# One decoder step on one core: small copies of the short convolution on GpSimd, softmax scaling on ScalarE, sampled attention's first loads placed earlier

## The chip, the core and the metric

The kernel is one program for one core of one Trainium2 chip. Its time is the device time of one execution, in microseconds (us), and the measure is the median of several executions. The engines are TensorE (PE in the profile, its weight loads PEld), VectorE (DVE), ScalarE (ACT), GpSimd (POOL) and SyncE (SP, which here only issues DMAs). Each runs its own queue in order and waits for the others by semaphores. All data are float32.

## What is computed

One inference step of one layer, for a prompt of 512 tokens and for 8 sequences with 4 new tokens each (32 rows), so 544 columns in all. Cut to what matters here:

```python
h = rms_norm(x, norm1_w) * (1 + scale1) + shift1
(z, xbc, dt, q, k, v, qi, ki, wi, gb, gc, hv, gates) = split(h @ w_in)
y_a, conv_new, ssm_h = ssd_mixer(z, xbc, ...)           # depthwise conv of 4 taps on xbc, SiLU, scan
y_b = attend(q, k, v, qi, ki, wi)                       # index scores, top-k keys, softmax + relative bias
u, sc_new = causal_dwconv(gc * hv, sc_prev, sc_conv_w)  # short conv: 3 taps, two old rows in front
y_c = gb * u
merged = sum(sigmoid(gate) * (y @ w_out))
...                                                     # residual, second norm, 32 experts, final norm
```

For the prompt the keys are the 512 tokens. For the new tokens they are 1024 old ones, kept in pages of 128 rows that a page table names, and the new ones. `sc_new` is the last two rows of `gc * hv` of each sequence, an output; so is `conv_new`, the last three rows of `xbc`.

## The kernel before

Activations lie transposed: 128 channels on the partitions, 544 columns (NT) along the row, of which 512 are the prompt and 32 the new tokens. `hT` holds the normed input as 8 such blocks. A weight tile (128 x 1024) holds the weights of 128 output channels; tiles come from HBM into a ring, in order, by SP.

**The long stage** makes the tiles of the short convolution (24: three for each of its eight groups m), of `xbc` (16) and of `z` (8). The first 40 are taken two at a time, w = 0 to 19 (`two_main`): four quarters of two tiles are multiplied by seven half products instead of eight, from sums of weights that POOL makes ahead (`weight_sum`, L384, four instructions of 128 x 512 for each w) and from sums of activations. Each half product is eight matmul rows in the profile (L362). ACT copies the first and the fifth product out (`first_out` L1063, `block_out` L1074 or L1076); DVE adds the others (`read_two` L1286, `read_four` L1266, `read_six` L1294, `read_seven` L1280). The seventh product, the last of a w, waits for `read_four`, since it takes the bank of PSUM that `read_four` frees. The z tiles (u = 40 to 47, `project`, L350) come one at a time.

In between stand other jobs, placed by hand by the number u of the tile (u = 2w and 2w + 1):

- Prompt attention: 32 units (query block, head), one at each tile from u = 6 (A0). Unit k: PE `qk` (L912) at u = k + 6; DVE `attend` adds mask and bias and takes the maximum (L1158, L1162, L1163); ACT exponentiates with the row's sum (L1135); DVE `normalise` at the next tile inverts the sum (L1169) and scales the row (L1170); PE `turn` (L921) transposes it one tile later, before the products of that tile; ACT copies out (L1123), PE `pv` (L932) multiplies.
- Selection on DVE: rounds of a maximum of 8 and a replacement (L1177, L1180), for the prompt at w = 0 to 6 and for the new tokens (32 x 1056 scores) from w = 7, as many for each w as `NEW_ROUNDS` says.
- The short convolution on DVE (`short`, L1212 to L1229), one group m after `read_two` of w = 2, 3, 5, 6, 8, 9, 11 and 12. It multiplies c and h into the row `cg` (L1212, L1215), copies the sequences' two old values in front (L1213), copies the new state out (L1217, L1218), then convolves (L1222, L1224) and multiplies by b (L1226, L1227).
- The convolution of `xbc` on DVE (L1196, L1199), with its prefixes and state copied by POOL (`fill_rows` L867 and L868, `save_rows` L877 and L878) and SiLU on ACT (L1096).
- The adaLN modulation on PE (L335) every sixth tile.

**Sampled attention** follows (PE L1434 to L1495). Two halves a of four sequences; 16 page units u of eight pages, K then V, in two buffers. Buffer 0 is loaded by SP, buffer 1 by POOL (`pages_in`), and unit 0 by POOL too. A load waits for `s_kvused`, the count of units used, which PE raises by 2 at the very start of this stage (so that the first two may come) and then by 1 for each unit. The page buffers lie where the last weight sums were. Between the units PE makes the short convolution's output products (`short_half`, L1434); ACT takes the sigmoid of their gate (L1511) and DVE multiplies (L1559). DVE begins the stage with a wait for the biases `snear`, which SP loads from `rel_dram` by four DMAs (L1394), after the convolution state, which lies in the same place, has been written out by ACT (L1144) at the end of the long stage.

## Time and profile before

| | us |
|---|---|
| median of 3 runs | 1441.66 |
| lowest, highest | 1440.3, 1447.06 |
| the profiled execution, its own time | 1446.04 |
| its span in the trace | 1444.3 |

| engine | busy us | share of the span |
|---|---|---|
| PE | 1306.4 | 90% |
| DVE | 765.9 | 53% |
| ACT | 234.6 | 16% |
| POOL | 254.9 | 18% |

The profile is of one execution. The long stage runs from about 180 us to 585 us, its z tiles from 520 us; sampled attention from 585 us to 740 us. A row of the timeline is a group of equal instructions: start, length (from the first's start to the last's end), engine, line, operation, output and input, shape, number; in brackets how long the engine stood idle before it and what released it. Where several engines wait in turn, the one with no idle row for long sets the pace. Instructions of one engine overlap a little, so the time that one takes from its engine is read from its start to the next one's start. PEclk is the granted clock of PE as a share of its full 2.4 GHz.

### The profile page before, as it was taken

The numbers are of one execution on the slowest core, as the hardware profiler recorded it, in microseconds if no ns is written. First come the engines' busy times: TensorE is split into PE (matmuls) and PEld (weight loads), VectorE is DVE, ScalarE is ACT, GpSimd is POOL, SyncE is SP. The second block draws the span as 40 slices with busy tenths as digits, with TensorE's granted clock in tenths as the row PEclk, the third lists the DMA queues.
The fourth block names the chain that finished last, engine by engine and source line by source line (L and its number), as shares of the span: only waits on it lengthen the run. The fifth ranks groups of instructions, "written<-read, shape, count | busy, mean of one in ns | idle before, by whom it ended". The sixth has DMA issues, their size and how long they took to land. (4 is left out here: it accounts for less than half of the span.)

```text
span 1444.3 us, 19365 instructions
## 1 busy us (share of the span) xinstructions
PE 1306.4 (90%) x6937; PEld 933.5 (65%) x6937; DVE 765.9 (53%) x1475; ACT 234.6 (16%) x514; POOL 254.9 (18%) x359
## 2 busy tenths in 40 slices
PE   5999999989999999999989988999999799787774
PEld 2787667667778778676767766888878633222223
DVE  1534689999988867010115557685567622111115
ACT  2201111111122222010122222410001300000001
POOL 0214333322423300321210002000001211111001
PEclk7899999999999999999999997999999889999995
DMA  9452233313323333655561111421245599999945
GB/s 368 154 109 86 89 126 117 117 59 117 117 77 111 114 104 104 204 177 176 181 226 44 30 44 72 167 73 59 88 132 251 194 404 419 419 420 419 419 175 186
DMA packets 65281, 250.87 MB, mean 174 GB/s; under 512 B 9802, under 2 KB 19434, under 8 KB 51978
## 3 DMA queue, kind: packets, MB, share of 16 engines
q1 hardware_dynamic: 48706, 213.40, 39.3%
q0 software_dynamic: 10112, 20.47, 4.2%
q10 hardware_dynamic: 6376, 15.83, 3.8%
q8 instruction: 56, 0.92, 0.3%
q14 instruction: 31, 0.25, 0.1%
HBM read 234.47 MB, written 22.91 MB: 178 GB/s over the span
## 5 line engine op out<-in xcount | busy, mean ns | idle before, releaser
L362 PE MATMUL psum<-arena 128*128 128x272 f32 x2184 | 517.4, 394 | 16.0 <-DVE arena L1266 12.5
L362 PEld LDWEIGHTS psum<-arena 128*128 128x128 f32 x2184 | 409.6, 189 | 119.7 <-issue 32.5
L384 POOL TENSOR_TENSOR arena<-arena 128x512 f32<-128x512 f32 x80 | 106.6, 1333 | 225.9 <-DMA arena<-in_weights 164.3
L2766 PE MATMUL psum<-arena 128*64 128x512 f32 x512 | 117.8, 605 | 24.5 <-DMA arena<-in_w_gu 22.1
L1434 PE MATMUL psum<-arena 128*128 128x272 f32 x512 | 123.1, 398 | 2.0 <-DVE arena L1559 2.0
L350 PE MATMUL psum<-arena 128*128 128x272 f32 x512 | 121.1, 397 | 1.0 <-DVE arena L2082 1.0
L1434 PEld LDWEIGHTS psum<-arena 128*128 128x128 f32 x512 | 96.4, 191 | 28.0 <-DVE arena L1559 6.5
L350 PEld LDWEIGHTS psum<-arena 128*128 128x128 f32 x512 | 98.0, 192 | 23.7 <-DVE arena L2082 1.7
L2766 PEld LDWEIGHTS psum<-arena 128*64 128x64 f32 x512 | 35.6, 136 | 96.0 <-issue 70.7
L2788 PE MATMUL psum<-arena 128*64 128x512 f32 x256 | 63.5, 640 | 18.9 <-issue 16.2
L1559 DVE TENSOR_TENSOR arena<-arena,psum 128x272 f32<-128x272 f32 x16 | 7.0, 439 | 136.3 <-ACT arena L1511 123.2
L2840 DVE TENSOR_TENSOR arena<-arena,psum 128x256 f32<-128x256 f32 x16 | 6.8, 422 | 133.1 <-ACT arena L2831 133.1
L1753 PE MATMUL psum<-arena 128*128 128x272 f32 x256 | 64.5, 406 | 2.9 <-PEq L206 2.9
L1180 DVE MATCH_REPLACE8 arena<-arena 32x1056 f32<-32x1056 f32 (+3 forms) x80 | 64.9, 817 | 0.0
L1177 DVE MAX8 arena<-arena 32x8 f32<-32x1056 f32 (+3 forms) x80 | 63.5, 827 | 1.3 <-DVE arena L745 0.3
L1753 PEld LDWEIGHTS psum<-arena 128*128 128x128 f32 x256 | 49.7, 198 | 13.6 <-issue 3.1
L2848 DVE TENSOR_SCALAR arena<-psum,arena 128x1024 f32<-128x1024 f32 x16 | 20.5, 1284 | 63.8 <-PE psum L2788 63.8
L592 POOL DMA_DIRECT2D arena<-in_pages_i x64 | 33.3, 521 | 118.9 <-issue 112.6
L384 DVE TENSOR_TENSOR arena<-arena 128x512 f32<-128x512 f32 x76 | 52.7, 693 | 2.6
L2731 POOL DMA_INDIRECT y_rows<-arena x16 | 16.0, 998 | 214.9 <-DVE arena L2848 214.9
L2788 PEld LDWEIGHTS psum<-arena 128*64 128x64 f32 x256 | 20.0, 145 | 52.4 <-issue 49.2
L2635 POOL TENSOR_TENSOR arena<-arena 128x544 f32<-128x544 f32 x6 | 9.3, 1544 | 228.0 <-ACT arena L2458 228.0
(381 smaller groups left out, 1504.7 us busy)
## 6 DMA issues: line engine op xcount, KB each, us to landing
arena<-in_weights SPq DMA_DIRECT2D x153, 512.0 KB, 4.6
arena<-in_w_gu SPq DMA_DIRECT2D x32, 2048.0 KB, 34.6
arena<-in_w_down SPq DMA_DIRECT2D x16, 2048.0 KB, 35.5
arena<-in_weights ACTq DMA_DIRECT2D x16, 512.0 KB, 4.1
arena<-in_pages_k POOLq DMA_DIRECT2D x40, 128.0 KB, 3.8
arena<-in_x SPq DMA_DIRECT2D x2, 2176.0 KB, 13.6
arena<-in_pages_v SPq DMA_DIRECT2D x32, 128.0 KB, 3.1
arena<-in_pages_v POOLq DMA_DIRECT2D x32, 128.0 KB, 3.3
```

What stands on the lines that cost most here:

```text
L350: mm = pe.matmul(out[:, h, :], lhsT=w_of(n, c), rhs=act[:, c, h * HALF:(h + 1) * HALF], start=(c == 0), stop=(c == DC - 1))
L362: mm = pe.matmul(out, lhsT=w[:, c * P:c * P + P], rhs=x[:, c, :], start=(c == 0 and not added), stop=(c == 3), skip_group_check=added or more)
L384: link(dve.tensor_tensor(sums[:, k], a, b, op))
L592: pool.dma_start(kidx[64 * a:64 * a + 64, bass.ds(b, 1), j * PAGE:(j + 1) * PAGE].rearrange("p a n -> p (a n)"), ins["pages_i"][bass.ds(of ...
L1177: dve.max(best8[0:s.shape[0], i, :], s).then_inc(s_top, 1)
L1180: dve.match_replace(s, best8[0:s.shape[0], i, :], s, CHOSEN).then_inc(s_top, 1)
L1434: mm = pe.matmul(psum[:, bank, 0:HALF], lhsT=w_of(n, c), rhs=act_of[:, c, h * HALF:(h + 1) * HALF], start=(c == 0), stop=(c == DC - 1))
L1753: mm = pe.matmul(psum[:, (2, 7)[k % 2], 0:HALF], lhsT=w_of(n, c), rhs=act_of[:, c, (k % 2) * HALF:(k % 2 + 1) * HALF], start=(c == 0), sto ...
L2731: pool.indirect_dma_start(out=y_rows, out_offset=bass.IndirectOffsetOnAxis(tab_i[:, p - XG:p - XG + 1], 0), in_=yst[:, k, :], in_offset=No ...
L2766: mm = pe.matmul(psum[CAP * e:CAP * e + CAP, 2 + k, :].rearrange("p (o f) -> p o f", o=2), lhsT=xgT[:, k, lo:lo + CAP], rhs=wv[:, e, c4], ...
L2788: mm = pe.matmul(psum[CAP * e:CAP * e + CAP, 4 + h, :], lhsT=actT[:, k, at:at + CAP], rhs=w_dn[:, e, f * D + h * 512:f * D + h * 512 + 512 ...
L2848: dve.tensor_scalar(yst[:, k, :].rearrange("p (a n) -> p a n", n=512), psum[:, 4:6, :], wtab[:, p:p + 1], None, ALU.mult).then_inc(s_yo, 1)
```

## The change

Three edits, and what they need:

1. **Short convolution.** The three small copies of `short` go to POOL. `prefix(m)` copies the old values in front of the row; DVE's product into the row waits for it (`s_cgpre`). `save_short(m)` copies the state out, after DVE has raised `s_cgrow` for the row; then POOL waits for the end of this `short` (`s_scd`) and makes the prefix of m + 2, which uses the same row buffer. Both stand in POOL's queue behind the weight sums of the next w. `s_fill` counts one less; ACT waits for the last state copy before it uses the buffers' place at w = 14.
2. **Probabilities.** `normalise` becomes `invert`: DVE keeps the reciprocal, ACT scales the row (an ACT copy with a scale for each partition), just before its exponential of the next unit, and raises `s_prob`. In `NEW_ROUNDS` one round moves from w = 17 to w = 19.
3. **Sampled attention.** PE raises `s_kvused` before tile 40 instead of at the start of the stage. ACT writes the convolution state at u = 43 instead of at the end, and asks for the biases itself at u = 46; SP does so no more.

```diff
+                def prefix(m):
+                    pool.tensor_copy(seq_new(cg[:, m % 2, :], SSEG_P, SSEG_S, 0, 2),
+                                     param("sc_prev").rearrange("p (m b k) -> p m b k", b=NB, k=2)[:, m]
+                                     ).then_inc(s_cgpre, 1)
+
+                def save_short(m):
+                    row = cg[:, m % 2, :]
+                    pool.wait_ge(s_cgrow, m + 1)
+                    pool.tensor_copy(sc_state[:, m, 0:2], row[:, SEQ:SEQ + 2])
+                    pool.tensor_copy(sc_state[:, m, 2:18].rearrange("p (b k) -> p b k", k=2),
+                                     seq_new(row, SSEG_P, SSEG_S, 4, 6)).then_inc(s_cgst, 1)
+                    if m + 2 < 8:
+                        pool.wait_ge(s_scd, m + 1)
+                        prefix(m + 2)
...
                     for i in range(4):
                         weight_sum(pool, main_tile(2 * w), sums_of(w), i, sum_link)
+                    if 0 < w - 1 <= XB_FIRST and (w - 1) % 3 != 1:
+                        save_short(2 * ((w - 1) // 3) - (0 if (w - 1) % 3 == 2 else 1))
...
+                pe.wait_ge(s_took3, 5 * N_SEVEN - 2)
+                pe.sem_inc(s_kvused, 2)
                 for u in range(2 * N_SEVEN, N_MAIN):
...
                     if w == HOME2:
                         act.wait_ge(s_scd, 8)
+                        act.wait_ge(s_cgst, 8)
...
+                    if 1 <= k <= NU:
+                        w = (A_UNITS[k - 1][0] + 1) * P
+                        act.wait_ge(s_esum, k)
+                        act.activation(sp4[:, (k - 1) % 3, 0:w], sp4[:, (k - 1) % 3, 0:w], ACT.Copy,
+                                       scale=esum[:, k - 1:k]).then_inc(s_prob, 1)
...
                     if u == 43:
                         queries_spread()
-                act.wait_ge(s_state, XBC)
-                act.dma_start(outs["conv"], conv_state).then_inc(s_convout, 16)
+                        act.wait_ge(s_state, XBC)
+                        act.dma_start(outs["conv"], conv_state).then_inc(s_convout, 16)
+                    if u == 46:
+                        act.wait_ge(s_convout, 16)
+                        for g in range(4):
+                            act.dma_start(snear[32 * g:32 * g + 32, :], slid(0, NS, 0, P + NS)).then_inc(s_nearl, 16)
...
-                def normalise(k):
-                    w = (A_UNITS[k][0] + 1) * P
-                    s = sp4[:, k % 3, 0:w]
+                def invert(k):
                     dve.wait_ge(s_exp, k + 1)
-                    link(dve.reciprocal(esum[:, k:k + 1], esum[:, k:k + 1]))
-                    dve.tensor_scalar(s, s, esum[:, k:k + 1], None, ALU.mult).then_inc(s_prob, 1)
+                    dve.reciprocal(esum[:, k:k + 1], esum[:, k:k + 1]).then_inc(s_esum, 1)
...
                     dve.wait_ge(s_first3, 2 * ((3 * m + 2) // 2) + 2)
-                    if m == 0:
-                        dve.wait_ge(s_fill, 1)
+                    dve.wait_ge(s_cgpre, m + 1)
                     dve.tensor_tensor(row[:, 2:2 + SEQ], c_[:, 0:SEQ], h_[:, 0:SEQ], ALU.mult)
-                    dve.tensor_copy(seq_new(row, SSEG_P, SSEG_S, 0, 2),
-                                    param("sc_prev").rearrange("p (m b k) -> p m b k", b=NB, k=2)[:, m])
                     link(dve.tensor_tensor(seq_new(row, SSEG_P, SSEG_S, 2, 6), by_seq(c_), by_seq(h_),
                                            ALU.mult))
-                    dve.tensor_copy(sc_state[:, m, 0:2], row[:, SEQ:SEQ + 2])
-                    dve.tensor_copy(sc_state[:, m, 2:18].rearrange("p (b k) -> p b k", k=2),
-                                    seq_new(row, SSEG_P, SSEG_S, 4, 6)).then_inc(s_cgst, 1)
+                    dve.sem_inc(s_cgrow, 1)
...
-                NEW_ROUNDS = (3, 2, 2, 3, 2, 2, 3, 3, 3, 3, 3, 2, 1)
+                NEW_ROUNDS = (3, 2, 2, 3, 2, 2, 3, 3, 3, 3, 2, 2, 2)
...
-                sp.wait_ge(s_convout, 16)
-                for g in range(4):
-                    sp.dma_start(snear[32 * g:32 * g + 32, :], slid(0, NS, 0, P + NS)).then_inc(s_nearl, 16)
...
-                pe.sem_inc(s_kvused, 2)
```

Below, the instructions as they stand in the engines' queues. `arena` is the whole SBUF buffer, `psum` all of PSUM; names in brackets are the semaphores waited for, by the program's names.

DVE, from `short` of w = 8 to the attention unit after it, before:

```order
L1212 TENSOR_TENSOR arena<-arena 128x512 [waits first_products_read3,products_read3]
L1213 COPY arena<-arena 128x8x2
L1215 TENSOR_TENSOR arena<-arena 128x8x4
L1217 COPY arena<-arena 128x2 [waits dve_link3]
L1218 COPY arena<-arena 128x16
L1222 TENSOR_SCALAR arena<-arena 128x560
L1224 SCALAR_TENSOR_TENSOR arena<-arena 128x560 [waits dve_link3] x2
L1226 TENSOR_TENSOR arena<-arena 128x512 [waits dve_link3]
L1227 TENSOR_TENSOR arena<-arena 128x32
L1286 TENSOR_TENSOR arena<-arena,psum 128x272 [waits dve_link3,half_products3]
L1266 TENSOR_TENSOR arena<-arena,psum 128x272 [waits products_read3]
L1169 RECIPROCAL arena<-arena 128x1 [waits exp_ready,products_read3]
L1170 TENSOR_SCALAR arena<-arena 128x256 [waits dve_link3]
```

and of the change:

```order
L1242 TENSOR_TENSOR arena<-arena 128x512 [waits sc_prefix_ready,first_products_read3,products_read3]
L1243 TENSOR_TENSOR arena<-arena 128x8x4
L1248 TENSOR_SCALAR arena<-arena 128x560 [waits dve_link3]
L1250 SCALAR_TENSOR_TENSOR arena<-arena 128x560 [waits dve_link3] x2
L1252 TENSOR_TENSOR arena<-arena 128x512 [waits dve_link3]
L1253 TENSOR_TENSOR arena<-arena 128x32
L1312 TENSOR_TENSOR arena<-arena,psum 128x272 [waits dve_link3,half_products3]
L1292 TENSOR_TENSOR arena<-arena,psum 128x272 [waits products_read3]
L1201 RECIPROCAL arena<-arena 128x1 [waits exp_ready,products_read3]
L1192 SCALAR_TENSOR_TENSOR arena<-psum,arena 128x256 [waits probs_turned,qk_ready]
```

The three copies and the scaling are gone; the convolution's scaling (L1248, before L1222) follows the row at once.

ACT in the z tiles, from u = 43 on, of the change (before, the two DMAs' places held nothing, and the state's DMA stood behind the last row):

```order
L1112 ACTIVATE arena<-arena 128x16 x15
L1174 DMA out_conv<-arena 128x432 [waits conv_state_saved]
L1105 ACTIVATE arena<-psum 128x544 [waits w_used]
L1121 ACTIVATE arena<-arena 128x568 [waits conv_state_saved,conv_ready] x2
L1105 ACTIVATE arena<-psum 128x544 [waits w_used]
L1121 ACTIVATE arena<-arena 128x568 [waits conv_state_saved,conv_ready] x2
L1105 ACTIVATE arena<-psum 128x544 [waits w_used]
L1121 ACTIVATE arena<-arena 128x568 [waits conv_state_saved,conv_ready] x2
L1178 DMA arena<-rel_dram 32x1x132 [waits conv_state_written]
L1178 DMA arena<-rel_dram 32x1x132 x3
L1105 ACTIVATE arena<-psum 128x544 [waits w_used]
L1154 ACTIVATE arena<-psum 128x512 [waits modulation_turned,w_used]
```

The state leaves three tiles before the biases are asked for, and both stand ahead of the last two tiles' outputs.

## Rows read from the trace of the kernel before

**Rows 1.** Waits of PE from 190 us on, then PE's timeline in the long stage.

```profile
PE psum L362 <- DVE arena L1266: 11.9, 8, 3.0
...
239.33 2.07 PE L362 MATMUL psum<-arena 128*128 128x272 f32 x8 [1.43 <-DVE arena L1266]
...
271.00 2.87 PE L362 MATMUL psum<-arena 128*128 128x272 f32 x8 [2.82 <-DVE arena L1266]
...
297.97 4.29 PE L362 MATMUL psum<-arena 128*128 128x272 f32 x16 [0.93 <-DVE arena L1294]
...
324.94 2.07 PE L362 MATMUL psum<-arena 128*128 128x272 f32 x8 [3.02 <-DVE arena L1266]
...
376.63 2.07 PE L362 MATMUL psum<-arena 128*128 128x272 f32 x8 [1.58 <-DVE arena L1266]
```

**Rows 2.** Windows: stretch, length, busy of each engine (count), granted clock, DMA.

```profile
272.00:277.00 5.00, 5.00 (x25) 1.91 (x24) 4.08 (x13) 0.78 (x3) 0.00 (x0) 0.66 0.36 102
```

**Rows 3.** Timeline of DVE in block w = 8.

```profile
316.92 1.33 DVE L1212 TENSOR_TENSOR arena<-arena 128x512 f32<-128x512 f32 x1
318.17 1.24 DVE L1213 COPY arena<-arena 128x16 f32<-128x16 f32 x1
...
319.54 1.21 DVE L1217 COPY arena<-arena 128x2 f32<-128x2 f32 x1
...
320.74 0.50 DVE L1222 TENSOR_SCALAR arena<-arena 128x560 f32<-128x560 f32 x1
321.27 1.64 DVE L1224 SCALAR_TENSOR_TENSOR arena<-arena 128x560 f32<-128x560 f32 x2
...
324.83 0.16 DVE L1169 RECIPROCAL arena<-arena 128x1 f32<-128x1 f32 x1
325.03 0.35 DVE L1170 TENSOR_SCALAR arena<-arena 128x256 f32<-128x256 f32 x1
325.30 0.42 DVE L1158 SCALAR_TENSOR_TENSOR arena<-psum,arena 128x256 f32<-128x256 f32 x1
```

**Rows 4.** Timelines: POOL's sums in w = 8; two DVE instructions elsewhere, under POOL.

```profile
315.08 5.64 POOL L384 TENSOR_TENSOR arena<-arena 128x512 f32<-128x512 f32 x4 [17.92 <-DMA arena<-in_weights]
...
217.74 2.53 DVE L1224 SCALAR_TENSOR_TENSOR arena<-arena 128x560 f32<-128x560 f32 x2
...
348.27 1.44 DVE L1170 TENSOR_SCALAR arena<-arena 128x256 f32<-128x256 f32 x1
```

**Rows 5.** Timeline of DVE: its idle rows, and a selection of w = 19.

```profile
277.35 0.29 DVE L1158 SCALAR_TENSOR_TENSOR arena<-psum,arena 128x128 f32<-128x128 f32 x1 [1.17 <-PE psum L912]
...
415.40 0.56 DVE L1158 SCALAR_TENSOR_TENSOR arena<-psum,arena 128x384 f32<-128x384 f32 x1 [0.55 <-PE psum L912]
...
506.22 1.23 DVE L1180 MATCH_REPLACE8 arena<-arena 32x1056 f32<-32x1056 f32 x1
...
517.56 0.44 DVE L1294 TENSOR_TENSOR arena<-arena,psum 128x272 f32<-128x272 f32 x1 [3.80 <-PE psum L362]
```

**Rows 6.** Timelines of PE at the start of sampled attention, and of POOL there.

```profile
596.25 1.85 PE L1464 MATMUL psum<-arena 128*32 128x256 f32 x16 [0.41 <-DMA arena<-in_pages_k]
600.08 9.13 PE L1434 MATMUL psum<-arena 128*128 128x272 f32 x32 [1.99 <-DVE arena L1559]
609.15 1.07 PE L1464 MATMUL psum<-arena 128*32 128x256 f32 x16
610.18 7.60 PE L1434 MATMUL psum<-arena 128*128 128x272 f32 x32
...
585.60 9.63 POOL L1380 DMA_DIRECT2D arena<-in_pages_k  x16 [63.64 <-PEq L1414]
```

**Rows 7.** Timeline of DVE at the start of sampled attention.

```profile
599.59 0.44 DVE L1559 TENSOR_TENSOR arena<-arena,psum 128x272 f32<-128x272 f32 x1 [13.07 <-DMA arena<-rel_dram]
```

**Rows 8.** Timeline of POOL: a prefix copy of `fill_rows`.

```profile
500.83 0.21 POOL L868 COPY arena<-arena 128x24 f32<-128x24 f32 x1
```

**Rows 9.** Timeline of ACT in block w = 8.

```profile
317.85 0.39 ACT L1123 ACTIVATE arena<-psum 128x256 f32<-128x256 f32 x1
```

More of the change, by code:

```diff
@@ L818, in build @@
             s_qz, s_qz0 = sem("q_spread"), sem("q_zeroed")
+            s_kvused = sem("pages_used")
+            s_nearl = sem("snear_loaded")
+            s_cgrow, s_cgpre = sem("sc_rows_ready"), sem("sc_prefix_ready")
+            s_esum = sem("sums_inverted")
+            snear = A.at(a_tmp + 4096 + KEYS + 1152, P + NS)
             qz = A.at(a_sc, KV, NB, 32)
@@ L879, in save_rows @@
                                          seq_new(xb[:, m, :], SEG_P, SEG_S, 4, 7)).then_inc(s_state, 1)
+                def prefix(m):
[11 more added lines that the diff above has]
+                        prefix(m + 2)
                 for i in range(2):
-                    last = pool.memset(cg[:, i, 0:2], 0.0)
-                last.then_inc(s_fill, 1)
+                    pool.memset(cg[:, i, 0:2], 0.0)
+                    prefix(i)
                 for w in range(N_SEVEN):
@@ L1190, in conv @@
                     if j in (0, 4, 12):
-                        dve.wait_ge(s_fill, {0: 2, 4: 3, 12: 4}[j])
+                        dve.wait_ge(s_fill, {0: 1, 4: 2, 12: 3}[j])
                     if j >= 2:
@@ L1245, in at_tile @@
                     if 1 <= k <= NU:
-                        normalise(k - 1)
+                        invert(k - 1)
                     if k == 0:
@@ L1349, in _ @@
                 gain_of(dve, link, 1, "norm2")
-            s_kvused, s_sl5, s_smax, s_sexp, s_sprob, s_st, s_stout, s_so, s_nearl = (sem(n) for n in (
-                "pages_used", "slogits_read", "smax_ready", "sexp_ready", "sprobs_ready",
-                "sprobs_turned", "sturned_out", "satt_out", "snear_loaded"))
+            s_sl5, s_smax, s_sexp, s_sprob, s_st, s_stout, s_so = (sem(n) for n in (
+                "slogits_read", "smax_ready", "sexp_ready", "sprobs_ready",
+                "sprobs_turned", "sturned_out", "satt_out"))
             s_kv0 = sem("first_pages_loaded")
@@ L1361, in build @@
             ptn = A.at(a_tmp + 4096 + KEYS + 1024, P, parts=NEW)
-            snear = A.at(a_tmp + 4096 + KEYS + 1152, P + NS)
             st5 = A.at(a_tmp + 4096 + KEYS + 1152 + P + NS, 4)
```

## The prediction

> **What bounds the kernel now.** I read the page first: TensorE (PE) is busy 90% of the span, so only its pauses can be won back. Then the timeline of PE through the long stage. It pauses inside blocks of two tiles, all but once before the last eight matmuls of a block: 1.08, 1.43, 2.82, 0.73, 0.93, 3.02, 1.09 and 1.58 us. L1294 of VectorE (DVE) releases the 0.93, L1266 the others and one of 0.15, 11.9 us in eight; five of the nine stand in [rows 1] as the pattern, beside that sum. Seven of the eight lie in blocks w = 2, 3, 5, 6, 8, 9, 11, which are the ones in which DVE does a `short`; the one of 0.93 us (w = 7) follows w = 6. After the pause of 2.82 us eight matmuls take 2.87 us, where the same eight take 2.07 us elsewhere, and the granted clock of 272 to 277 us is 0.66 (of 2.4 GHz; 1.0 around it): 5 x 0.34 = 1.7 us, of which I count 1.6 [rows 1, 2].
>
> The timeline of DVE says why. From 278 us to 415 us it has no idle row at all [rows 5]: DVE paces this stretch and PE waits for it whenever it falls behind. In `short` of w = 8, L1212 starts at 316.92 and the row sum is done only at 324.8 [rows 3]. Two tiny copies stand out: L1213 (128x16) takes 1.24 us and L1217 (128x2) 1.21 us, as long as one POOL sum of the weights, of which four run from 315.08 to 320.72 [rows 3, 4]. So the copies do not cost work, they wait for POOL's running instruction. POOL slows others too: L1224 twice takes 2.53 us under it and 1.64 us without, and the probabilities' scaling L1170 takes 1.44 us under it and 0.35 us without [rows 3, 4].
>
> The third view is PE at the start of sampled attention: it waits 0.41 us for pages and 1.99 us for DVE's L1559, which itself waited 13.07 us for the biases from `rel_dram`; around these pauses the clock is low (16 page matmuls 1.85 us instead of 1.07, 32 others 9.13 us instead of 7.60) [rows 6, 7].
>
> **The copies of `short` (eight times).** Off DVE go L1213, L1217 and L1218. From the start of L1213 to that of L1222 (318.17 to 320.74) [rows 3] are 2.57 us, of which L1215 keeps some 0.2, so 2.4 us at most. But the next instruction on DVE is now L1222, a scaling of SBUF data as L1170 is, and L1170 under POOL took 1.1 us more [rows 4]. I replay w = 8, in us from POOL's start, with its four sums ending at 1.3, 2.7, 4.0 and 5.3 or so. L1212 ends at 3.1 as now; L1222 waits until the third sum is done (4.0), runs to 4.5; the first L1224 shares its time with the fourth sum (+0.9, as in [rows 4]) and ends at 6.15, the second at 6.95. Now it ends at 321.27 + 1.64 - 315.08 = 7.8. The saving is 0.9 us, not 2.4. POOL's starts lie 0.8 to 3.4 us before L1212 in the other blocks, and the replay gives 0.8 to 1.0 for each. I take 0.9, with 0 (everything is passed on) and 2.4 as bounds.
>
> Here a rule of the Trainium skill bears on it, in SBUF — State Buffer, "Who interferes with whom": DVE and GpSimd share one pair of ports, a lock held for a whole instruction by whoever comes first, and copies, tensor_scalar and tensor_tensor with both inputs in SBUF all want it. The rows above agree (a 128x2 copy of 1.21 us). By that rule the edit only takes away customers of the lock, not the lock; a reader who prices the copies at their busy time would write 2.4 us per `short`.
>
> The copies on POOL cost it 0.21 us each by their nearest likes (L868, same shape but for the width) [rows 8]: 0.6 us for three, in a queue that stands idle 17.92 us before its next sums [rows 4]. Queued behind POOL's new waits (for the row, for the end of `short`) are the next weight sums; they start only when their tiles have landed and PE has finished two blocks back, after `short` is over. DVE's new wait, for the prefix, is met one `short` earlier. Zero on the path.
>
> **Scaling moved to ACT (32 times).** Off DVE goes the step L1169 to L1158: 324.83 to 325.30, 0.47 us, of which the reciprocal's own slot of 0.11 stays: 0.36 us [rows 3]. Narrow units give less (0.3), wide ones more. Two of them ran under POOL (the 1.44 of [rows 4] and one like it at the start of w = 4): 1.1 us more each. On ACT the scaling costs about what L1123 costs at the same width, 0.39 us [rows 9], and ACT is busy 16% of the span by the page. The path that could suffer is PE's transpose, which now waits for ACT: L1169 ends at 324.99, ACT +0.4, handing over +0.14, so 325.6; PE, released at 324.94 with 2.07 us of matmuls before the transpose [rows 1, 3], comes at 327.0. 1.4 us of slack, zero cost.
>
> **The sum in the long stage.** While DVE never idles, PE gains what DVE has saved since its last idle, but no more than the pauses so far.
> - w = 2: min(1.08, 0.9) = 0.9.
> - w = 3 and 5: DVE saves 0.9 + 0.9 + four scalings 1.4 + 1.1 contended = 4.3; PE can gain 0.9 at w = 3 and then 2.82: 3.7. The clock's dip goes with the long pause: 1.6.
> - w = 6 to 11, from DVE's idle at 277.35 [rows 5]: by w = 8 saved 2 x 0.9 + 4 x 0.36 = 3.2 (pauses so far 4.7); by w = 9 another 0.9 + 0.7 = 4.9; by w = 11 DVE has 8.3, PE gains 4.9 + 1.58 = 6.4.
> Together 12.6 us. With 2.4 per `short` all pauses go: 12.7 + 1.6 = 14.3. With 0 per `short`: 2.5 + 1.6 for w = 5 and 2.2 + 1.6 = 3.8 for the rest, 7.8 in all.
>
> The one selection round that moves from w = 17 to w = 19 costs nothing: it is a maximum and a replacement over 1056 scores, 1.23 us each or a little more [rows 5], 2.6 us in front of a DVE idle of 3.80 us [rows 5]; from w = 12 on PE has no pauses.
>
> **Pages and biases.** `s_kvused` is raised before tile 40, so POOL's sixteen page loads (9.63 us of issue [rows 6]) no longer wait 63.64 us for PE but start near 522 us, behind POOL's last copies; sixty microseconds cover them, and the buffers are free by the waits that stand before them. POOL's issues now run beside DVE's convolutions and may slow those; their results are due a tile later, and TensorE's eight tiles there have no pause for them. The convolution state is written at u = 43 and the biases asked for at u = 46, both on ACT's queue: four issues between one tile's output and the next, with a whole tile of PE to spare before anyone waits for ACT. SP loses four issues and a wait and comes to its pages earlier. PE's 0.41 + 1.99 go, and with them the clock's loss, 0.78 + 1.53 [rows 6]: 4.7 us. What comes late next is the second page unit's load by SP, released when unit 0 is done; before PE needs it come unit 1 and two halves of the short product, 7.6 us each [rows 6].
>
> **Sum.** 12.6 + 4.7 = 17.3 us. Of the profiled execution's own 1446.04 us 1428.7 are left. That execution lies 4.4 us over the median of the runs shown (1441.66); on the median's scale it is 1424.4 us.
>
> **Rivals.**
> - *Everything goes*: the copies' full 2.4 us are won since L1222 finds POOL no hindrance (for it: L1222 took 0.50 us each time so far [rows 3]; against it: L1170's 1.44). 14.3 + 4.7 = 19.0, 1422.7 us.
> - *The wait is passed on*: L1222 and both L1224 take over what the copies waited. For it speaks that POOL's four sums are as long as before and DVE's queue is full of instructions that they slow. 7.8 + 4.7 = 12.5, 1429.2 us. By the rule of SBUF — State Buffer in the Trainium skill, taken to its end, this is the case.
> - *Another wait at the start of sampled attention*: PE's pauses there stay, because ACT's queue or POOL's descriptors deliver late. 12.6 only, 1429.1 us.
> - *Slower*: PE's transposes wait for ACT. Each of 32 now has the chain reciprocal, ACT's scaling, PE, and ACT works in order, behind its own waits for PE's products. It decides once the chain passes 2.0 us where it is now some 0.6; at 1.2 us over, 32 x 1.2 = 38 us less the 17.3 gained give 1463 us. Against it: ACT is mostly idle in this stretch (L1123 of w = 8 is its last work for 8 us), and what stands ahead of the scaling on it has been released earlier.
> - *It does not do what it says* for the pages: POOL stays behind another wait. The order of its queue shows only the counters named, so this goes with the third.
>
> **How the numbers follow.** Forecast (1424.4) 0.57; everything goes 0.13; passed on 0.15; attention's pauses stay 0.08; slower 0.04, and no change to speak of, several of these at once, 0.03. The range holds the first four: from 1422.7 less 2 us, since the runs shown spread from 1440.3 to 1447.06, to 1429.2 and 2 us: 1420.5 to 1431.5. A measurement of this kernel can tell about 0.5% (7 us) from no change. Faster 0.92, same 0.04, slower 0.04.
>
> **What would show it.** Right: L1222's successor taking 1 to 1.5 us in several `short`s; PE pauses in the long stage of 1 to 3 us in all, none over 2; no low clock near 270 and 600 us; page loads from 522 us; DVE's wait for `rel_dram` gone; ACT's new scalings 0.3 to 0.6 us. Wrong: PE waiting for ACT's scaling before transposes; L1222 always at 0.50; pauses at new places, at w = 4 or 10; or a PE wait for pages of unit 0 or 2.

## The result and the profile after

The changed kernel takes 1438.07 us (median of 10 runs, 1431.3 to 1444.16) beside 1447.09 us for the kernel before in the same comparison (10 runs, 1440.3 to 1450.49): a ratio of 0.9943, interval 0.992 to 0.9966, so some 8 us (5 to 12) instead of the 17.3 forecast, and a time outside the range of 1420.5 to 1431.5 us. The profiled execution took 1438.11 us, its span is 1436.5 us; of before they were 1446.04 and 1444.3.

Where the 7.8 us between the two spans lie, by the first instruction of each stretch on PE:

| stretch | before | after | forecast | measured |
|---|---|---|---|---|
| start to the last product of w = 0 | 189.18 | 188.15 | 0 | -1.03 |
| from there to the first z matmul (long stage) | 330.90 | 327.72 | -12.6 | -3.18 |
| z tiles and sampled attention | 222.48 | 219.01 | -4.7 | -3.47 |
| the rest | 701.74 | 701.62 | 0 | -0.12 |

These are single profiled executions. A second one of the changed kernel (e8 below) has 326.61 us in the long stage, 217.56 in the third row and 706.99 in the rest, so the two gains measured lie between 3.2 and 4.3 us and between 3.5 and 4.9.

**PE's timeline in the long stage**, its rows that begin with idle time (start, length, instructions, in brackets the idle time and what ended it):

```profile
221.10 2.07 PE L362 MATMUL psum<-arena 128*128 128x272 f32 x8 [0.93 <-DVE arena L1292]
237.90 2.07 PE L362 MATMUL psum<-arena 128*128 128x272 f32 x8 [1.19 <-DVE arena L1292]
269.07 2.07 PE L362 MATMUL psum<-arena 128*128 128x272 f32 x8 [2.31 <-DVE arena L1292]
286.83 2.07 PE L362 MATMUL psum<-arena 128*128 128x272 f32 x8 [1.49 <-DVE arena L1292]
295.11 3.98 PE L362 MATMUL psum<-arena 128*128 128x272 f32 x16 [0.87 <-DVE arena L1320]
...
321.06 2.81 PE L362 MATMUL psum<-arena 128*128 128x272 f32 x8 [2.31 <-DVE arena L1292]
...
372.31 2.07 PE L362 MATMUL psum<-arena 128*128 128x272 f32 x8 [0.84 <-DVE arena L1292]
```

Nearly the pattern of [rows 1] is left, eight pauses of nine, 10.10 us in all where 12.83 were. Block by block: w = 2 gained 0.15, w = 3 0.24, w = 5 0.51, w = 7 0.05, w = 8 0.71, w = 9 all its 1.09, w = 11 0.74; w = 6 lost 0.76. Block by block this is not the edits' doing alone. The kernel e1 below has the instructions of before throughout this stage, and its profile shows 1.98 us of pause at w = 6 where before shows 0.73, and none at w = 7 and w = 9 (PE's timeline of e1, its rows from 285 to 345 us that begin with idle time):

```profile
288.36 3.58 PE L362 MATMUL psum<-arena 128*128 128x272 f32 x8 [1.98 <-DVE arena L1277]
...
324.11 2.07 PE L362 MATMUL psum<-arena 128*128 128x272 f32 x8 [3.08 <-DVE arena L1277]
```

**DVE's and POOL's timelines in block w = 8**, which answer to [rows 3, 4]:

```profile
313.00 0.69 DVE L1242 TENSOR_TENSOR arena<-arena 128x512 f32<-128x512 f32 x1
313.60 1.26 DVE L1243 TENSOR_TENSOR arena<-arena 128x32 f32<-128x32 f32 x1
315.01 1.45 DVE L1248 TENSOR_SCALAR arena<-arena 128x560 f32<-128x560 f32 x1
316.50 2.53 DVE L1250 SCALAR_TENSOR_TENSOR arena<-arena 128x560 f32<-128x560 f32 x2
319.07 0.69 DVE L1252 TENSOR_TENSOR arena<-arena 128x512 f32<-128x512 f32 x1
...
311.66 5.93 POOL L384 TENSOR_TENSOR arena<-arena 128x512 f32<-128x512 f32 x4 [17.37 <-DMA arena<-in_weights]
```

The waiting copies are gone, and two other instructions wait in their stead: the 128x32 product L1243 (L1215 before) takes 1.26 us instead of 0.18, the scaling L1248 (L1222 before) 1.45 us instead of 0.50. By shape, over all eight `short`s (DVE's groups of 205 to 400 us: busy us, mean ns of one, idle):

```profile
L1250 DVE SCALAR_TENSOR_TENSOR arena<-arena 128x560 f32<-128x560 f32 x16 | 16.4, 1025 | 0.6
L1248 DVE TENSOR_SCALAR arena<-arena 128x560 f32<-128x560 f32 x8 | 10.7, 1342 | 1.2 <-DVE arena L1243 0.2
L1243 DVE TENSOR_TENSOR arena<-arena 128x32 f32<-128x32 f32 x8 | 10.1, 1258 | 0.0
```

Best measured is the stretch from the start of the row's product (L1212, now L1242) to the start of the multiplication by b (L1226, now L1252), read from the timeline in each of the eight blocks w = 2, 3, 5, 6, 8, 9, 11, 12:

| kernel | us in each block | sum |
|---|---|---|
| before | 6.27, 5.65, 6.63, 5.41, 6.02, 6.36, 5.48, 4.79 | 46.6 |
| after | 6.11, 5.43, 6.98, 6.16, 6.07, 4.50, 6.07, 5.34 | 46.7 |

Three copies less, and the eight blocks are no shorter. The sums repeat within about 1 us: e1, with the copies, has 46.6 us again, e8, without them, 47.7. A single block varies more, with the moment at which DVE meets POOL's sums. w = 9 is 1.9 us shorter than before, and its pause is gone, but e1 has 5.42 us there and no pause either. w = 6 is 0.75 us longer, and its pause grew by 0.76, but e1 has 6.28 us there: in before this row's product starts 2.5 us behind POOL's first sum, in e1 1.3 us and in the changed kernel 1.5 us. There three instructions in a row wait (DVE's timeline, then POOL's):

```profile
278.67 1.66 DVE L1242 TENSOR_TENSOR arena<-arena 128x512 f32<-128x512 f32 x1
280.26 1.25 DVE L1243 TENSOR_TENSOR arena<-arena 128x32 f32<-128x32 f32 x1
281.66 1.46 DVE L1248 TENSOR_SCALAR arena<-arena 128x560 f32<-128x560 f32 x1
...
277.16 5.65 POOL L384 TENSOR_TENSOR arena<-arena 128x512 f32<-128x512 f32 x4 [8.98 <-DMA arena<-in_weights]
```

**Start of sampled attention**, timelines of PE, POOL and DVE:

```profile
591.55 1.66 PE L1483 MATMUL psum<-arena 128*32 128x256 f32 x16
593.14 8.66 PE L1453 MATMUL psum<-arena 128*128 128x272 f32 x32
...
525.51 9.68 POOL L1405 DMA_DIRECT2D arena<-in_pages_k  x16 [7.77 <-issue]
...
589.54 0.44 DVE L1578 TENSOR_TENSOR arena<-arena,psum 128x272 f32<-128x272 f32 x1 [7.24 <-ACT arena L1530]
```

And windows of the changed kernel (length; busy of PE, PEld, DVE, ACT, POOL with counts; granted clock; DMA share, GB/s):

```profile
267.00:272.00 5.00, 2.93 (x20) 1.76 (x24) 4.68 (x16) 1.18 (x4) 0.42 (x3) 1.00 0.00 0
321.00:327.00 6.00, 5.94 (x28) 2.76 (x29) 4.38 (x9) 1.39 (x4) 0.00 (x0) 0.72 0.33 85
592.00:605.00 13.00, 13.00 (x70) 9.24 (x63) 0.44 (x1) 0.40 (x1) 1.36 (x3) 0.87 0.42 126
```

Both pauses of [rows 6] are gone, the loads start 60 us earlier, and DVE waits no longer for `rel_dram` [rows 7]. But PE's first matmuls are slow still (1.66 for 1.07 us, 8.66 for 7.60): the clock was low here without any pause right before them (the last idle row of PE is 0.72 us at 580.51, and e1 and e8 have it too). In the long stage the low clock moved from w = 5 [rows 2] to w = 8; in e1 it comes behind the 1.98 us at w = 6 and not behind the 3.08 at w = 8, and in e8 not at all (1.00), with a pause of 2.49 us at w = 8.

### The profile page after: what moved, and what is told of

Read it like the earlier page. It is cut to its first block and busy times, and to the rows that moved or that the text cites. A ratio compares the mean times of both kernels' runs of the same rounds, so it can differ in the third digit from the quotient of the medians.

```text
span 1436.5 us, 19374 instructions
## 1 busy us (share of the span) xinstructions
PE 1303.0 (91%) x6937; PEld 929.0 (65%) x6937; DVE 749.8 (52%) x1419; ACT 250.2 (17%) x546; POOL 261.2 (18%) x383
## 5 line engine op out<-in xcount | busy, mean ns | idle before, releaser
L1772 PEld LDWEIGHTS psum<-arena 128*128 128x128 f32 x256 | 49.9, 199 | 13.7 <-issue 3.2
```

What stands on the lines that cost most here:

```text
L1772: mm = pe.matmul(psum[:, (2, 7)[k % 2], 0:HALF], lhsT=w_of(n, c), rhs=act_of[:, c, (k % 2) * HALF:(k % 2 + 1) * HALF], start=(c == 0), sto ...
```

## The experiments

Times are medians; ratios are to the kernel before, run beside each. L is the long stage, P the sum of PE's pauses in it from w = 2 on, S the z tiles and sampled attention, as in the table above. These three come from one profiled execution each. The kernel before was run anew with each set of experiments (medians 1447.55, 1445.89 and 1448.10), so the ratios and not the times are to be compared.

| kernel | us | ratio (95%) | L | P | S |
|---|---|---|---|---|---|
| before | 1447.09 | | 330.90 | 12.83 | 222.48 |
| after | 1438.07 | 0.9943 (0.992 to 0.9966) | 327.72 | 10.10 | 219.01 |
| e1_pages | 1443.35 | 0.9967 (0.995 to 0.9985) | 330.03 | 12.13 | 217.50 |
| e2_short | 1445.85 | 0.9987 (0.9964 to 1.001) | 330.05 | 12.21 | 224.64 |
| e3_scale | 1444.69 | 0.9982 (0.9964 to 1.0) | 328.93 | 11.42 | 221.70 |
| e4_late_sums | 1423.86 | 0.9845 (0.9801 to 0.9888) | 313.91 | 0.00 | 219.71 |
| e5_late_sums_old | 1434.54 | 0.9921 (0.9891 to 0.9951) | 317.57 | 2.54 | 223.95 |
| e6_late_pages | 1430.25 | 0.9881 (0.9849 to 0.9913) | 317.55 | 2.53 | 220.95 |
| e7_late_again | 1428.02 | 0.9872 (0.9847 to 0.9897) | 313.92 | 0.00 | 220.79 |
| e8_after_again | 1441.34 | 0.9957 (0.9937 to 0.9977) | 326.61 | 10.37 | 217.56 |
| e11_late_short | 1430.48 | 0.9872 (0.9849 to 0.9894) | 317.10 | 2.19 | 224.00 |
| e12_late_scale | 1431.21 | 0.9859 (0.982 to 0.9899) | 313.99 | 0.00 | 223.36 |

### Each edit alone

**e1_pages**: the third edit alone (the biases' part not shown).

```diff
+                pe.wait_ge(s_took3, 5 * N_SEVEN - 2)
+                pe.sem_inc(s_kvused, 2)
                 for u in range(2 * N_SEVEN, N_MAIN):
...
-                pe.sem_inc(s_kvused, 2)
```

> Only the third edit (pages and biases early), the rest as before. Measures in this and the other runs: L, the long stage, from the end of the pause of w = 0 to the first z matmul (before 330.9 us, after 327.7), the sum P of PE's pauses in it from w = 2 on (before 12.8, after 10.1), and S, from the first z matmul to the first matmul behind sampled attention (before 222.5, after 219.0). Theory (the three edits act in places of their own): L 330.9 and P 12.8 stay, S falls to 219.0. Rival (the loads in the z tiles disturb or help the long stage's end, or S needs the other edits): L moves by over 1 us or S stays above 221.

S falls by 5.0 us, both pauses are gone, and here the clock stays full (the same window as above, of e1):

```profile
592.00:605.00 13.00, 13.00 (x80) 9.20 (x79) 0.88 (x2) 0.40 (x1) 0.55 (x2) 1.00 0.36 102
```

Priced at 4.7, worth 5.0 where the clock stays up, and 1.5 us better than the 219.0 expected, which was the changed kernel's. L is 0.87 us and P 0.7 us less than in before, though no instruction of the long stage differs: so much two executions can differ there, and smaller differences in L or P prove nothing as long as POOL's sums run beside the `short`s. In the changed kernel the same stretch shows 3.5, and the difference is (1.66 - 1.07) + (8.66 - 7.60) = 1.65 us of slower matmuls. The same kernel run again (e8) has the clock at 1.00 there and S lower by 4.9.

**e2_short**: the first edit alone.

```diff
-                dve.tensor_copy(sc_state[:, m, 0:2], row[:, SEQ:SEQ + 2])
-                dve.tensor_copy(sc_state[:, m, 2:18].rearrange("p (b k) -> p b k", k=2),
-                                seq_new(row, SSEG_P, SSEG_S, 4, 6)).then_inc(s_cgst, 1)
+                dve.sem_inc(s_cgrow, 1)
...
+                    if 0 < w - 1 <= XB_FIRST and (w - 1) % 3 != 1:
+                        save_short(2 * ((w - 1) // 3) - (0 if (w - 1) % 3 == 2 else 1))
```

> Only the first edit (small copies of the short convolution on POOL). Theory (the wait for POOL's running sum is passed on): the 128x32 product takes 1.26 us instead of 0.18 and the scaling behind it 1.46 instead of 0.50, each short is at most 0.5 us shorter, P falls from 12.8 to 11 to 12.5. Rival (the copies gave most of the gain of the long stage, the scaling nothing): P 10 to 10.5, L 328.

P falls by 0.6 and L by 0.85 us where the forecast had 0.9 for each of eight. That is no more than e1 shows with nothing changed there. The eight stretches take 45.4 us instead of 46.6: 0.15 us each; the whole 1.2 us is hardly more than the 1 us by which such sums repeat. The wait came as expected: in all eight blocks the 128x32 product takes 1.25 to 1.26 us. The kernel's time can't be told from that of before.

**e3_scale**: the second edit alone.

```diff
-                    dve.tensor_scalar(s, s, esum[:, k:k + 1], None, ALU.mult).then_inc(s_prob, 1)
+                    dve.reciprocal(esum[:, k:k + 1], esum[:, k:k + 1]).then_inc(s_esum, 1)
```

> Only the second edit (probabilities scaled by ACT, one selection round moved). Theory (only what is saved inside a block with a short counts, some 0.4 us for each of six such blocks; what is saved in others becomes DVE idle before the next unit's logits): P falls from 12.8 by 2 to 3, to 10 to 11, and DVE shows new idle rows for PE's qk of 1 to 2.5 us in blocks without short. Rival (DVE paces the whole stretch, savings add up, as predicted): P falls by 5 to 8. Second rival (scaling on ACT gives nothing): P stays at 12.5 to 12.8.

L falls by 1.97 us, P by 1.41, so P misses the 2 to 3 expected, and of L 0.87 may be chance (e1). The interval of the time reaches 1. ACT does the work at 399 to 716 ns by width, and PE never waits for it before a transpose. But 32 scalings of 0.36 us would be 11.5 us of DVE. That they are not had is seen in DVE's idle rows. The kernel before has no idle row of DVE between 238.27 and 277.35 us, where [rows 5] begin. e3 has three there, 1.50, 0.84 and 0.17 us, and the changed kernel nearly the same; these are its rows:

```profile
248.66 0.44 DVE L1312 TENSOR_TENSOR arena<-arena,psum 128x272 f32<-128x272 f32 x1 [1.50 <-PE psum L362]
255.21 0.29 DVE L1192 SCALAR_TENSOR_TENSOR arena<-psum,arena 128x128 f32<-128x128 f32 x1 [0.85 <-PE psum L934]
273.79 0.29 DVE L1192 SCALAR_TENSOR_TENSOR arena<-psum,arena 128x128 f32<-128x128 f32 x1 [0.17 <-PE psum L934]
```

What DVE saves in w = 3 and 4 it now spends waiting for PE, ahead of the `short` of w = 5, whose length then sets the pause as before. Further on it is the same: before has no idle row from 277.35 to 415.40 us, the changed kernel has three there (and e3 2.41, 2.05 and 0.83 us):

```profile
327.95 0.43 DVE L1192 SCALAR_TENSOR_TENSOR arena<-psum,arena 128x256 f32<-128x256 f32 x1 [2.40 <-PE psum L934]
359.17 0.56 DVE L1192 SCALAR_TENSOR_TENSOR arena<-psum,arena 128x384 f32<-128x384 f32 x1 [2.10 <-PE psum L934]
377.90 0.56 DVE L1192 SCALAR_TENSOR_TENSOR arena<-psum,arena 128x384 f32<-128x384 f32 x1 [0.83 <-PE psum L934]
```

In e8, where the clock stays full at w = 8, the first of them is 0.77 us: part of the 2.40 is DVE waiting for a PE that is slow. In e3 the eight stretches are even a little longer, 47.6 us.

### GpSimd's sums kept out of the way

**e4_late_sums**: the changed kernel, but POOL makes the next weight sums only when the `short` beside which they ran is over. No DVE or ACT work is touched.

```diff
+                    if 0 < w - 1 <= XB_FIRST and (w - 1) % 3 != 1:
+                        m = 2 * ((w - 1) // 3) - (0 if (w - 1) % 3 == 2 else 1)
+                        save_short(m)
+                        pool.wait_ge(s_scd, m + 1)
                     for i in range(4):
                         weight_sum(pool, main_tile(2 * w), sums_of(w), i, sum_link)
-                    if 0 < w - 1 <= XB_FIRST and (w - 1) % 3 != 1:
-                        save_short(2 * ((w - 1) // 3) - (0 if (w - 1) % 3 == 2 else 1))
```

> The changed kernel with POOL's weight sums held back in the eight blocks with a short until that short is over (POOL saves the state rows first, then waits for the end of short, then sums). Theory (a lock between the two engines costs the time): in short the product 0.18, the scaling 0.50, the two convolution steps 1.64 and the row product 0.69 in all eight, a short some 3 us shorter than after (4.3 instead of 7 us), P falls from 10.1 to under 4, with at most 1 us of new pauses where PE waits for POOL's sums; L 320 to 323. Rival (DVE's own work bounds the blocks, not the contention): P 8 to 10, L 327. Second rival (held-back sums come late): new pauses before the second or fourth product of the next block of over 1 us each, P above 10.

Timelines of DVE and POOL in w = 8:

```profile
321.40 0.69 DVE L1244 TENSOR_TENSOR arena<-arena 128x512 f32<-128x512 f32 x1
322.01 0.18 DVE L1245 TENSOR_TENSOR arena<-arena 128x32 f32<-128x32 f32 x1
322.34 0.51 DVE L1250 TENSOR_SCALAR arena<-arena 128x560 f32<-128x560 f32 x1
322.89 1.64 DVE L1252 SCALAR_TENSOR_TENSOR arena<-arena 128x560 f32<-128x560 f32 x2
324.56 0.69 DVE L1254 TENSOR_TENSOR arena<-arena 128x512 f32<-128x512 f32 x1
...
325.63 5.39 POOL L384 TENSOR_TENSOR arena<-arena 128x512 f32<-128x512 f32 x4
```

DVE's groups by shape, as above:

```profile
L1245 DVE TENSOR_TENSOR arena<-arena 128x32 f32<-128x32 f32 x8 | 1.5, 184 | 0.0
L1250 DVE TENSOR_SCALAR arena<-arena 128x560 f32<-128x560 f32 x8 | 4.1, 515 | 1.2 <-DVE arena L1245 0.2
```

And PE's only wait from 189 to 503 us (total, times, longest), which is that of w = 0:

```profile
PE psum L362 <- DVE arena L1294: 0.6, 1, 0.6
```

Each stretch takes 3.16 to 3.18 us, 25.3 us for the eight instead of 46.7. PE has no pause left and L falls by 13.8 us, much more than the expectation had (320 to 323 for the 313.91 measured): the 10.10 of pauses, 1.6 us of low clock at w = 8 (eight products 2.81 instead of 2.07, the modulation after them 2.81 instead of 1.93), and some 2 us that show as the same matmuls being busy less long. Nobody waits for the later sums. This kernel is faster than both others; run again beside the changed one (e7 and e8) the intervals stay apart, 0.9847 to 0.9897 against 0.9937 to 0.9977.

> The changed kernel with held-back sums once more, timed in five rounds. Both theories of the mechanism expect its ratio to the kernel before at 0.980 to 0.987; if the first measurement of 0.9845 owed much to chance, 0.988 to 0.994.

> The changed kernel itself, unaltered, timed on the same chip as the others, for its clock and its pauses in a second profiled execution. Theory (the low clock at the start of sampled attention comes in some executions and not in others, whether or not PE pauses there): P 9.5 to 10.7 again, L 326 to 328.5, but S anywhere from 217 to 220. Rival (the low clock belongs to this kernel's order of work): S 219 again, with 8.6 us for the second run of 32 products instead of 7.6.

e7 comes out between its two expectations, e8 as its theory had it: pauses and L again (10.37 and 326.61 us), and S 217.56 us with a full clock.

**e5_late_sums_old**: the kernel before, with that wait alone. **e6_late_pages**: e5 and the third edit.

```diff
+                    if 0 < w - 1 <= XB_FIRST and (w - 1) % 3 != 1:
+                        m = 2 * ((w - 1) // 3) - (0 if (w - 1) % 3 == 2 else 1)
+                        pool.wait_ge(s_scd, m + 1)
                     for i in range(4):
                         weight_sum(pool, main_tile(2 * w), sums_of(w), i, sum_link)
```

> The kernel before with one edit alone: POOL's weight sums in the eight short blocks wait for the end of short. The small copies and the scaling stay on DVE, pages and biases stay late. Theory (it is the meeting of the two engines that costs, not who does the copies): each copy takes 0.17 us (some 1.2 before), L1224 0.80 each, a short is under 5 us, P falls from 12.8 to under 2, L from 330.9 to 313 to 316. Rival (the edits of the change are needed too, the gain of the held-back sums rests on the copies being off DVE): the two copies keep 1.2 us each, P 5 to 8, L 320 or more.

> The kernel before with the held-back sums and the third edit (pages and biases early), the copies and the scaling still on DVE. Theory: within 1 us of the changed kernel with held-back sums in L (313 to 315) and S (217 to 220): the first two edits then bring nothing. Rival: they still bring 2 us or more, L 316 or more.

The one wait takes 13.3 us from L, three to four times what the three edits of the change together took (3.2 and 4.3 us in its two profiles). e5's pauses (2.54 us for under 2) and its L (317.57 for 313 to 316) come out a little over what was expected. e6 misses its expectation that the first two edits bring nothing once the sums are held back: its L is 317.55 us and that of e4 313.91, as its rival had it. The copies with which the prediction began cost this (e5, groups by shape):

```profile
L1220 DVE COPY arena<-arena 128x2 f32<-128x2 f32 x8 | 1.4, 170 | 0.3
L1216 DVE COPY arena<-arena 128x16 f32<-128x16 f32 x8 | 1.4, 170 | 0.0
```

The eight stretches take 26.2 us. So 46.6 - 26.2 = 20.4 us in before, 2.55 us each, were waits for POOL. They show in the length of the copies, of the row's product and of the convolution, but go with POOL's sums, not with the copies. e6 adds 3.0 us in S. It is not the 5.0 of e1, for here and in e7 the granted clock is low in two later places of this stage, 0.57 from 637 to 641 and from 650.5 to 654.5 us in e6, 2 x 4 x 0.43 = 3.4 us, where e1 has 1.00.

**e11_late_short** and **e12_late_scale**: that wait with the first edit alone, and with the second alone. The edits are those of e2 and e3 with those of e4 and e5.

> The first edit alone (the three copies on GpSimd), with the weight sums held back until the short block is over. Beside the kernel before with held-back sums (pauses 2.54 us from w = 2 on, of which 1.80 + 0.32 at w = 6; long stage 317.57 us), the copies cost DVE 0.17 us each there, 0.5 us for each short block. Theory A (a block wins only what it has saved within itself): the pause at w = 6 falls to 1.3, the small ones go, long stage 316.7 to 317.0. Theory B (savings add up from block to block while DVE never idles): w = 6 is the third short block since w = 2 and has 1.5 to 2.0 us, so all pauses go and the long stage is at 314 to 315 us. Either way the edit is worth at least as much as it was under GpSimd's sums (0.85 us).

> The second edit alone (scaling on ScalarE), with the weight sums held back until the short block is over. Beside the kernel before with held-back sums (pauses 2.54 us, long stage 317.57). Theory A (within the block only): w = 6 holds at most two scalings ahead of its last product, so its pause falls from 1.8 to some 1.1 to 1.4, long stage 316.8 to 317.2. Theory B (savings add up): nine scalings of narrow units lie between w = 2 and w = 6, 2.5 to 3 us in all, so all pauses go and the long stage is at 314 us as with all edits.

With POOL out of the way L repeats to 0.02 us (317.57 in e5 and 317.55 in e6, 313.91 in e4 and 313.92 in e7), so small differences can be read. The first edit is worth 0.47 us (the eight stretches 25.4 for 26.2, 0.1 us each where 0.5 was expected), less than the 0.85 that was to be the least. The second is worth 3.58 us, nearly all of the 3.66 that the two bring together (e4). So e11 is close to theory A, savings count within a block only, and e12 at theory B, they add up. DVE and POOL in block w = 6, and PE's matmuls there, first of e5, then of e12 (with DVE's idle rows ahead of the block):

```profile
278.98 10.77 POOL L384 TENSOR_TENSOR arena<-arena 128x512 f32<-128x512 f32 x8 [10.85 <-DVEq L1232]
...
280.56 1.18 DVE L1165 TENSOR_TENSOR arena<-arena 128x128 f32<-128x128 f32 x1
...
288.65 0.44 DVE L1297 TENSOR_TENSOR arena<-arena,psum 128x272 f32<-128x272 f32 x1
...
289.15 2.11 PE L362 MATMUL psum<-arena 128*128 128x272 f32 x8 [1.80 <-DVE arena L1297]
```

```profile
249.15 0.44 DVE L1296 TENSOR_TENSOR arena<-arena,psum 128x272 f32<-128x272 f32 x1 [1.34 <-PE psum L362]
255.69 0.29 DVE L1171 SCALAR_TENSOR_TENSOR arena<-psum,arena 128x128 f32<-128x128 f32 x1 [0.85 <-PE psum L920]
271.72 0.29 DVE L1171 SCALAR_TENSOR_TENSOR arena<-psum,arena 128x128 f32<-128x128 f32 x1 [1.32 <-PE psum L920]
...
282.18 0.29 DVE L1175 TENSOR_TENSOR arena<-arena 128x128 f32<-128x128 f32 x1
...
289.33 0.44 DVE L1304 TENSOR_TENSOR arena<-arena,psum 128x272 f32<-128x272 f32 x1
...
286.52 7.60 PE L362 MATMUL psum<-arena 128*128 128x272 f32 x32
```

From `read_seven` ahead of the `short` (274.16 in e5, 276.13 in e12) to the `read_six` that releases PE, DVE takes 14.49 us in e5 and 13.20 in e12 (1.29 less), of which 0.89 is the wait of L1165 for a sum (1.18 for 0.29) that e12 doesn't meet. PE's 16 or 32 products start 9.26 us after the first point in e5 and 10.39 in e12: 1.13 us are brought along from earlier blocks. 1.29 + 1.13 = 2.42, for a pause of 1.80 and 0.55 us now to spare. (PE makes this pause in the products of w = 7, waiting for `read_six` of w = 6; it is the one of 0.93 us in before.) So savings do carry from block to block, as far as DVE was behind; what goes beyond that becomes one of the idle rows.

**e9_scale_in_short** and **e10_scale_elsewhere**: e3, but ACT scales only the 7 units whose scaling stands in a block with a `short`, ahead of it, or only the other 25. Each was executed once (1445.16 and 1449.69 us, beside 1446.08 for before), so only L and P are read.

```diff
+            ON_ACT = [(not (j + 7) & 1 and (j + 7) // 2 in SHORT_BLOCKS) == True for j in range(NU)]
...
-                    if 1 <= k <= NU:
+                    if 1 <= k <= NU and ON_ACT[k - 1]:
```

> The second edit for seven units alone: ACT scales only the units whose turn on DVE comes in the first tile of a block with a short (w = 3, 5, 6, 8, 9, 11, 12), ahead of that short; all else as in the run with scaling alone (P 11.4, L 328.9). Theory (only what DVE saves between the unit's logits and the end of short shortens a pause): nearly the whole effect of all 32, P 11.4 to 12.0. Rival (savings add up over the whole stretch): a fifth of it, P 12.5.

> The complement: ACT scales the other 25 units, the seven stay on DVE. Theory: P 12.3 to 12.9, as in the kernel before, and DVE idle rows for PE's qk of 2 us in blocks without short. Rival: P 11.5 to 11.8, four fifths of the effect.

| ACT scales | L | P |
|---|---|---|
| none (before) | 330.90 | 12.83 |
| 7 in blocks with a `short` | 329.58 | 11.54 |
| the 25 others | 329.28 | 11.76 |
| all 32 (e3) | 328.93 | 11.42 |

Either part alone wins 1.3 to 1.6 us of L, both together 2.0. The parts don't add up, and e1 won 0.87 with no scaling moved: neither expectation can be told from the other, and this doesn't tell how the gain splits. While POOL's sums run beside the `short`s, each shift of DVE by some tenths changes which instruction meets a sum, and that noise is as large as what was to be split.

## Why the prediction was wrong

**What bounds the kernel: right.** PE waits for DVE in the blocks with a `short`, and what holds DVE is POOL's running sum. e4 and e5 show it: with the sums elsewhere 13.3 to 13.8 us go.

**The copies, 0.9 us in each of eight: wrong, and the main step that failed.** The measured saving of the stretches is nothing (46.6 to 46.7), and 0.15 us each with this edit alone. The replay let only L1222 wait, once, and took over L1215 at its 0.2 us. But L1215 was quick by its place. Of POOL's four sums in w = 8 here are the fourth of before and the third of the changed kernel (POOL's timeline):

```profile
319.45 1.27 POOL L384 TENSOR_TENSOR arena<-arena 128x512 f32<-128x512 f32 x1
...
314.89 1.27 POOL L384 TENSOR_TENSOR arena<-arena 128x512 f32<-128x512 f32 x1
```

In before L1215 starts at 319.33, at once behind the copy L1213 that had waited, and ahead of this sum; L1217 comes behind the sum's start (319.54) and waits. As L1243 (313.60) the product is the first to meet a running sum and waits 1.26 us. L1248, which waits for its result, starts at 315.01, when POOL's next sum has begun, and waits again. Two waits went and two came in six of the eight blocks (in w = 9 L1248 finds no sum, and in w = 12 L1217 had found none before). That the order of starts decides this is read from the rows and was not tried by itself; that the waits are POOL's doing is shown by e4, where both are gone. The rule of the Trainium skill that the prediction named (SBUF — State Buffer, "Who interferes with whom") was the better guide: it also says that a DVE instruction with two SBUF inputs contends with a GpSimd one that reads SBUF, which is L1243, a product of two SBUF tiles. The prediction repeats this, but its replay left the product out. The runs agree, 1.26 us under POOL and 0.18 without (e4). *The wait is passed on* is what happened to the copies, though to the product and the scaling rather than to the scaling and both L1224; it had a chance of 0.15 and should have had most.

**Savings add up while DVE never idles: half right.** They carry (e12 against e5), but only as long as DVE is behind. The prediction read from [rows 5] that DVE had no idle row and took that for a stretch in which any saving counts. With 0.36 us for each scaling and the 1.1 us twice, DVE caught up with PE in w = 3 to 5 and then waited for it, 1.50 + 0.85 us at 248 and 255 us; w = 5 won 0.51 of the 2.8 counted. From w = 8 on it met 2.40, 2.10 and 0.83 us more. This is why even the rival with nothing for the copies (7.8 us in the long stage; its own parts, 2.5 + 1.6 + 3.8, give 7.9) was too high for the 3.18 measured: the working capped each block's gain by the pauses so far, but not by what idle time DVE would meet. By the prediction's own sums, of the 9.4 us missing in this stage 12.6 - 7.8 = 4.8 are the copies, 1.6 the clock and the remaining 3 this step; no run splits them exactly.

**Scaling on ACT costs PE nothing: right.** The slower rival did not occur; ACT's scalings took 0.40 to 0.72 us. **The moved round and POOL's copies: right**, no pause behind w = 11 and no wait of DVE for the prefix.

**Pages and biases, 4.7 us: the mechanism right, the clock's share not sure.** The pauses of 2.4 us went in every kernel with this edit. The 2.3 us for the clock came in e1 and e8 and two thirds of it not in the profiled execution of the change. Over all fourteen profiles the low clock at the start of this stage is there in each of the eight without the edit, and in two of the six with it (the change and e4), where it costs about half. So removing the pauses helps, but not each time.

**The clock's dip in the long stage, 1.6 us: wrong as a term of the sum.** The pause of 2.82 us shrank only to 2.31, and the dip there went all the same; a dip came at w = 8 (0.72 from 321 to 327 us), behind a pause that was shorter than before. In e8, the same kernel, the pauses are alike and no dip comes. The six profiles with held-back sums all have a full clock in this stage. Taking away a pause does not take away its dip one for one.

**From the profiled execution to the median, 4.4 us: wrong.** The median of three runs (1441.66) was low; over ten it is 1447.09, so the profiled 1446.04 was an ordinary one. Without this step the forecast would have been 1428.7. Of the 13.7 us between 1424.4 and 1438.07, 5.4 lie in this median and 8.3 in the gain.

Against the marks set down ahead: L1222's successor at 1.45 to 1.47 us, loads from 525.5 us, no wait for `rel_dram`, ACT at 0.4 to 0.7 us came; pauses of 1 to 3 us in all, none over 2, did not (10.10, two of 2.31). A full clock near 270 us came, one near 600 us did not (0.87 from 592 to 605 us), and the dip at w = 8 is at a new place. They tell more than the marks intended: the successor took its 1.45 us or more in all blocks but one, and its predecessor 1.25 to 1.28 in all of them.

## What to carry to other kernels

An instruction that waits for another engine's running instruction can show the wait as its own length, but the wait belongs to the other engine's queue: taking the instruction away can hand the wait to the next one that meets it, as here. Before moving such work, look at what the other engine runs at that moment and whether it could run elsewhere; here one semaphore wait on GpSimd, whose sums had time to spare, gave 13.3 us in the long stage where three edits gave 3.2 to 4.3. (The ratios of the whole times, 0.9921 and 0.9943, have intervals that overlap; with the wait added to the change they stay apart, 0.9872 and 0.9957.) And before a difference between two profiles is put down to an edit, look at a kernel that leaves the same stretch alone: e1 moved single pauses by over 1 us without an edit there. And a saving counts at most as far as the engine is behind: an engine without idle rows may get them as soon as something is saved.

## What was not expected of the hardware

- VectorE and GpSimd side by side are far from sharing evenly: four sums of 128x512 take GpSimd 5.7 us beside a `short` (the mean of the eight in before, 5.64 to 6.03) and 5.33 to 5.40 without (e4 and e5), some 0.4 us more, while the `short` takes 2.55 us more. The small VectorE instructions that wait, down to 128x2 elements, take 1.2 to 1.3 us, the scaling 1.45 and a convolution step 1.69, about as long as one sum or a little more (5.39 / 4 = 1.35).
- In the changed kernel PE's clock was low at the start of sampled attention (0.57 from 591.5 to 595.5 us, 0.87 from 592 to 605) with PE busy the whole window; in e1 and e8, equally busy, it was 1.00. What sets it apart was not tried.
- The stages behind sampled attention, which no kernel here touches, took between 697.1 and 707.0 us over the fourteen profiles. With that, single runs tell nothing of edits worth 2 to 5 us, and the long stage had to be compared by its own length.
